# Attention by pairs of heads: a block mask carried in extra contraction rows, probabilities normalised before they are turned, values stationary on two column halves

## The reference

```python
for blk in range(S // Q_BLOCK):                       # Q_BLOCK = 128, CHUNK = 64
    q0 = blk * Q_BLOCK
    k_end = q0 + Q_BLOCK
    s = einsum('bqhd,bkhd->bhqk', q[:, q0:k_end], k[:, :k_end]) * scale
    mask = (arange(k_end) // CHUNK)[None, :] <= ((q0 + arange(Q_BLOCK)) // CHUNK)[:, None]
    s = where(mask, s, -inf)
    p = softmax(s, axis=-1)
    outs.append(einsum('bhqk,bkhd->bqhd', p, v[:, :k_end]))
```

## Time and profile before

| what | value |
|---|---|
| median of 3 runs | 4078.86 us (4068.8 to 4081.03) |
| span of the profiled execution, its only recorded time | 4081.4 us |
| TensorE busy in the span | 3546.4 us (87%) |
| VectorE busy | 1301.3 us (32%) |
| ScalarE busy | 776.8 us (19%) |
| mean granted TensorE clock | 0.926 |

### The profile page before, as it was taken

The page is one execution under the profiler, slowest core; times in us unless marked ns, Lnnn a source line. Parts: engine busy times, 40 slices in busy tenths (PEclk is TensorE's granted clock), DMA queues, the critical chain, the costliest instruction groups (busy, mean ns, idle before and its releaser), DMA issues. The chain is left out here.

```text
span 4081.4 us, 40264 instructions
## 1 busy us (share of the span) xinstructions
PE 3546.4 (87%) x12609; PEld 1976.0 (48%) x12610; DVE 1301.3 (32%) x1923; ACT 776.8 (19%) x1214; POOL 329.9 (8%) x600
## 2 busy tenths in 40 slices
PE   5999599979999996999778986947999999999862
PEld 2444255547676444444357762534444444444421
DVE  2222233344343123111246662253111111111155
ACT  2222123333333001111122220211111111111102
POOL 3100000000000000111110000001111111111042
PEclk9999799979898997999989998968999999999986
DMA  6910201221111210999631001106778977767474
GB/s 238 371 36 26 109 26 42 57 72 42 32 42 30 74 74 34 378 367 368 225 91 27 21 0 66 37 16 236 280 271 307 333 275 277 274 245 277 156 254 158
DMA packets 204249, 636.98 MB, mean 156 GB/s; under 512 B 35349, under 2 KB 97401, under 8 KB 167033
## 3 DMA queue, kind: packets, MB, share of 16 engines
q1 hardware_dynamic: 142808, 412.34, 28.8%
q0 software_dynamic: 43488, 158.35, 10.5%
q10 hardware_dynamic: 17856, 65.02, 3.9%
HBM read 492.00 MB, written 143.65 MB: 156 GB/s over the span
## 5 line engine op out<-in xcount | busy, mean ns | idle before, releaser
L1560 PE MATMUL gu_ps<-w_gu,x_t 128*128 x2016 | 891.0, 595 | 6.5 <-DVE x_t L1617 3.4
L1560 PEld LDWEIGHTS gu_ps<-w_gu,x_t 128*128 128x128 f32 x2016 | 375.9, 191 | 432.3 <-issue 432.3
L1581 PE MATMUL y_ps<-w_dn,hid_t 128*128 x992 | 446.3, 592 | 0.0
L390 PE MATMUL ps<-second,wcol 128*128 128x512 f32 x768 | 333.2, 596 | 9.9 <-DMA wcol<-in_w_in_dram 7.5
L1615 DVE TENSOR_TENSOR hid<-act_g,gu_ps 128x256 f32<-128x256 f32 x126 | 53.0, 421 | 873.7 <-ACT act_g L1597 873.7
L1581 PEld LDWEIGHTS y_ps<-w_dn,hid_t 128*128 128x128 f32 x992 | 179.1, 191 | 177.9 <-issue 177.9
L390 PEld LDWEIGHTS ps<-second,wcol 128*128 128x128 f32 x768 | 146.8, 191 | 195.4 <-issue 187.6
L1520 POOL COPY idx<-moe_slot_tok 128x1 int32 (+1 forms) x128 | 23.2, 181 | 2646.4 <-POOLq L94 1450.2
L1602 ACT ACTIVATE y<-y_ps 128x1024 f32<-128x1024 f32 x124 | 126.9, 1023 | 497.4 <-PE y_ps L1581 497.4
L1597 ACT ACTIVATE act_g<-gu_ps 128x256 f32<-128x256 f32 x126 | 48.4, 384 | 793.4 <-PE gu_ps L1560 793.4
L1545 PEld LDWEIGHTS x_ps<-ident,xb 128*128 128x128 f32 x1024 | 133.5, 189 | 91.4 <-issue 60.8
(11 more groups left out here) (406 smaller groups left out, 4127.3 us busy)
## 6 DMA issues: line engine op xcount, KB each, us to landing
w_gu<-in_w_gate_dram SPq DMA_DIRECT2D x96, 1024.0 KB, 8.0
w_gu<-in_w_up_dram SPq DMA_DIRECT2D x96, 1024.0 KB, 11.0
w_dn<-in_w_down_dram SPq DMA_DIRECT2D x96, 1024.0 KB, 13.4
expert_out<-y ACTq DMA_DIRECT2D x124, 512.0 KB, 9.7
expert_out<-zero POOLq DMA_DIRECT2D x94, 512.0 KB, 37.7
wcol<-in_w_in_dram SPq DMA_DIRECT2D x12, 1024.0 KB, 9.7
qk_by_head<-stage SPq DMA_DIRECT2D x32, 384.0 KB, 3.3
qk<-qk_by_head SPq DMA_DIRECT2D x16, 768.0 KB, 5.2
```

What stands on the lines that cost most here:

```text
L390: last = nc.tensor.matmul(ps[:, slot, c, h * BANK:(h + 1) * BANK], wcol[:, k, kc, c * P:(c + 1) * P], G.u[:, kc, h * BANK:(h + 1) * BANK], ...
L1560: last = nc.tensor.matmul(gu_ps[:, slot], x_t[:, slot, c, :], w_gu[:, bass.ds(ws, 1), :, c, :].rearrange("p o g n -> p (o g) n"), start=c ...
L1581: last = nc.tensor.matmul(y_ps[:, h * BANK:(h + 1) * BANK], hid_t[:, slot, c, :], w_dn[:, bass.ds(ws, 1), c, h * BANK:(h + 1) * BANK] .rea ...
```

## The change

Only `attention` changes, and its two neighbours are left alone.

1. The mask's matmul is gone. Eight rows are added below the 96 of queries and keys (`KROWS` = 104). Row r holds, on the query side, 1 for the first 64 queries of tile r and, on the key side, 1e30 for the last 64 keys of block r, and 0 elsewhere. GpSimd writes these rows at the start of the stage into all four buffers of `qk`: two fills and 16 selects. TensorE waits for all 18 before its first scores.
2. Heads are taken in pairs, tile by tile: wide of head A, narrow of A, wide of B, narrow of B. Scores of a wide tile are issued four steps ahead, of a narrow one two steps ahead. `qk` has four buffers (was two), values are loaded by pairs, `prob` and `prob_t` have more buffers.
3. VectorE normalises the probabilities before they are turned: a reciprocal of the step's sum and a multiply in place over the tile (`scale`), and TensorE's turn waits for it. The scaling, turning and copying of `o_rows` is gone.
4. In `values` the 64 value columns of a head are stationary and 128 turned queries move. Head A writes output partitions 0 to 63, head B 64 to 127, and their matmuls alternate. The result is already turned; ScalarE copies it to `G.yb` in two pieces per pair.

```diff
-            n = (ORDER[s % T] + 1) * P
+            n = (tile_of(s) + 1) * P
...
         def _(pool):
-            nc.gpsimd.memset(early[:, 0:CHUNK], 1.0).then_inc(cleared, 1)
-            nc.gpsimd.memset(early[:, CHUNK:], 0.0).then_inc(cleared, 1)
-            nc.gpsimd.memset(hide[:], -NEG).then_inc(cleared, 1)
+            g = nc.gpsimd
+            st = Steps(pool, cleared)
+            st(g.memset(qk[QK:KROWS, :, 0, :], 1.0))
+            st(g.memset(qk[QK:KROWS, :, 1, :], -NEG))
+            st.join()
+            for u in range(4):
+                for side, first in ((0, 0), (1, CHUNK)):
+                    x = qk[QK:KROWS, u, side, :]
+                    st(g.affine_select(out=x, in_=x, compare_op=ALU.is_ge, fill=0.0, base=-first,
+                                       pattern=[[1, S]], channel_multiplier=-P))
+            st.join()
...
-            pe.wait_ge(cleared, 3)
+            pe.wait_ge(cleared, 18)
...
-                        nc.tensor.matmul(out[:, c0:c0 + w], qk[:, u % 2, 0, t * P:(t + 1) * P],
-                                         qk[:, u % 2, 1, c0:c0 + w], start=True, stop=c0 + w < n)
-
-                    nc.tensor.matmul(out[:, n - CHUNK:n], early[:], hide[:], start=False, stop=True
-                                     ).then_inc(sc_ready, 1)
+                        last = nc.tensor.matmul(out[:, c0:c0 + w], qk[:, h % 4, 0, t * P:(t + 1) * P],
+                                                qk[:, h % 4, 1, c0:c0 + w], start=True, stop=True)
+                    last.then_inc(sc_ready, 1)
...
-                    pe.wait_ge(exp_done, j * N + (s + 1))
+                    pe.wait_ge(scaled, j * N + (s + 1))
...
                     for b in range(t + 1):
-                        last = nc.tensor.matmul(o_ps[:, t, :], prob_t[:, s % 2, b, :],
-                                                vv[:, u % 2, b, :], start=b == 0, stop=b == t)
+                        for a, of in ((0, s - 2), (1, s)):
+                            rows = slice(a * VH, (a + 1) * VH)
+                            last = nc.tensor.matmul(o_ps[rows, r, :], vv[:, p % 2, b, rows], turned_of(of)[:, b, :],
+                                                    start=b == 0, stop=b == t)
                     last.then_inc(o_ready, 1)
...
-                scores(0)
-                scores(1)
+                for s in range(3):
+                    scores(s)
                 for i in range(N):
                     turn_probs(i)
-                    if i + 2 < N:
-                        scores(i + 2)
-                    if i:
+                    if ahead(i) < N:
+                        scores(ahead(i))
+                    if i and (i - 1) % 4 >= 2:
                         values(i - 1)
-                    for kind, p in turns[b_no["probs", i] + 1:][:1]:
-                        if kind == "out" and i + 1 < N:
-                            turn_out(p)
                 values(N - 1)
-                turn_out(ROUND // 2 - 1)
...
+                def scale(s):
+
+                    one = slice(s % 8, s % 8 + 1)
+                    v.wait_ge(exp_done, j * N + (turn_no[s] + 1))
+                    d.reciprocal(inv[:, one], total[:, one]).then_inc(inv_ready, 1)
+                    v.wait_ge(inv_ready, j * N + (s + 1))
+                    d.tensor_scalar(prob_of(s), prob_of(s), inv[:, one], None, ALU.mult).then_inc(scaled, 1)
+
+                for s in range(3):
+                    tops(s)
+                scale(0)
+                for i in range(N):
+                    v.wait_ge(b_ready, j * N + (i + 1))
+                    if i >= 8:
+                        v.wait_ge(o_ready, j * VALS + (value_no(i - 8) + 1))
+                    t = tile_of(i)
+                    if i % 2 == 0:
+                        d.tensor_copy(turned_of(i)[:, 4:t + 1, :], turn_b[:, 0:t - 3, :]).then_inc(b_taken, 1)
+                        scale(i + 1)
+                        if i + 2 < N:
+                            scale(i + 2)
                     else:
-                        d.tensor_copy(prob_t[:, n % 2, 0:t + 1, :], turn_b[:, 0:t + 1, :]).then_inc(b_taken, 1)
-                    if n + 2 < N:
-                        tops(n + 2)
+                        d.tensor_copy(turned_of(i)[:, 0:t + 1, :], turn_b[:, 0:t + 1, :]).then_inc(b_taken, 1)
+                    if ahead(i) < N:
+                        tops(ahead(i))
```

More of the change, by code:

```diff
@@ L812, in attention, with head_of, tile_of, ahead @@
     ORDER = [7, 0, 6, 1, 5, 2, 4, 3]
+    PAIRS = ROUND // 2
     N = ROUND * T
[L815 to L824, removed]
-    with ph.ctx:
[L826 to L835, removed]
+    KROWS = QK + T
+    OUTS = 2 * PAIRS
+    VALS = PAIRS * T
+    def head_of(s):
+        return s // (2 * T) * 2 + s // 2 % 2
+    def tile_of(s):
+        return ORDER[s % (2 * T) // 4 * 2 + s % 2]
+    def ahead(s):
+        return s + 4 if s % 2 == 0 else s + 2
+    scored = [0, 1, 2] + [ahead(s) for s in range(N) if ahead(s) < N]
+    turn_no = {s: n for n, s in enumerate(scored)}
+    assert sorted(scored) == list(range(N))
+    with ph.ctx:
+        qk = ph.sb("qk", [KROWS, 4, 2, S])
+        vv = ph.sb("vv", [P, 2, T, 2 * VH])
+        prob_l = ph.sb("prob_l", [P, 2, S])
+        prob_s = ph.sb("prob_s", [P, 2, BANK])
+        prob_tl = ph.sb("prob_tl", [P, 4, T, P])
+        prob_ts = ph.sb("prob_ts", [P, 4, T // 2, P])
+        shift = ph.sb("shift", [P, 8])
+        total = ph.sb("total", [P, 8])
+        inv = ph.sb("inv", [P, 8])
         wide = ph.ps("wide", [P, 2, S])
@@ L878, in _ @@
+            for p in range(2):
+                for a in range(2):
+                    load(2 * p + a, 2 * p + a)
+                load_values(p, p)
             with sp.Fori(0, ROUNDS - 1) as j:
[L879 to L882, removed]
+                for p in range(PAIRS):
+                    reload(j, p)
+            for p in range(PAIRS - 2):
+                reload(ROUNDS - 1, p)
@@ L890, in _ @@
+            st.join()
+            for u in range(4):
+                for side, first in ((0, 0), (1, CHUNK)):
+                    x = qk[QK:KROWS, u, side, :]
+                    st(g.affine_select(out=x, in_=x, compare_op=ALU.is_ge, fill=0.0, base=first + CHUNK - 1,
+                                       pattern=[[-1, S]], channel_multiplier=P))
+            assert st.n == 18
         @block.tensor
         def _(pe):
-            pe.wait_ge(cleared, 3)
+            pe.wait_ge(cleared, 18)
@@ L917, in turn_probs @@
                         blocks = blocks[4:]
-                    pe.wait_ge(b_taken, 1 + j * B_ALL + b_no[what])
+                    pe.wait_ge(b_taken, 1 + j * N + s)
                     for b, src in enumerate(blocks):
@@ L935, in values @@
                     last.then_inc(o_ready, 1)
-                def turn_out(p):
-                    what = ("out", p)
-                    pe.wait_ge(o_taken, 1 + j * ROUND + (p + 1) * 2)
-                    pe.wait_ge(a_taken, 1 + j * A_ALL + a_no[what])
-                    for b in range(4):
-                        last = nc.tensor.transpose(turn_a[:, b, :], o_rows[:, b, :], G.ident[:])
-                    last.then_inc(a_ready, 1)
-                    pe.wait_ge(b_taken, 1 + j * B_ALL + b_no[what])
-                    for b in range(4):
-                        last = nc.tensor.transpose(turn_b[:, b, :], o_rows[:, 4 + b, :], G.ident[:])
-                    last.then_inc(b_ready, 1)
```

152 lines of the change are left out of this document (68 added, 84 removed).

## The result

| | before | after |
|---|---|---|
| median | 4079.95 us (4068.8 to 4091.2, 4 runs) | 3964.26 us (3961.66 to 3966.53, 4 runs) |
| stage, first scores to last copy to `yb` | 880.0 to 1321.5: 441.5 us | 898.0 to 1206.0: 308.0 us |
| a pair of heads at full clock | 49.9 us | 35.3 us |

The account below looks back on a forecast made before the run. TensorE, in its own program order, was taken to bound the attention stage. 8 x 37.2 + 12 (rounds) + 27 (clock) + 24 (start) = 361 us against 441.5, so -81: 3998 us, range 3970 to 4066.

Parts of the forecast that it names:

- eight pairs: Attention stage, eight pairs of heads at full clock: 37.2 us each after the change, where one took 49.88.
- two rounds, 12: Start and end of each of two rounds, with empty queues and last tiles uncovered: 6 us a round, where it was 3.
- half clock, 27: Time at 1.2 GHz in the changed stage: 61 us of it, losing 27 us.
- the start: TensorE waits for GpSimd's 18 mask-row writes before first scores: +24 us, bounds +18 and +39.
- The clock: I keep the share of half-clock time: Whole stage: half-clock share stays at 0.18, 79 of 441.5 us before, so 61 us at half lose 27.
- the case in which it stays away: Half clock absent from the stage but for its first 10 us: forecast 22 us lower, 3976.
- the walk: Waits followed along the engines' queues through all 16 steps of a pair: TensorE waits 3.0 us a pair.
- Side by side: Values product: the two column halves run beside each other, 7.7 us a pair in place of 15.4; chance 0.50.
- halves in turn: Values product: halves follow each other, 0.107 us a pass, 43.3 us a pair, 4048 us; chance 0.30 including partial overlap.
- The masks: Mask matmuls after the scores, 16 a pair at 0.56 us: removing them saves 9.0 us a pair.
- the lower bound, +18: Low end for the later first scores, which wait for GpSimd's fills and selects; +24 us was taken.
- slower by the clock: Rival for the stage: TensorE's longer gaps bring half clock oftener, up to 4217 us if all at half; chance 0.10.

## Why the prediction was wrong, step by step

The forecast gave 361 us for start and stage together, from 880; it took 326.0. The 35 us of the miss (34 between the forecast and the median), by terms:

| term of the sum | forecast | measured | off by |
|---|---|---|---|
| eight pairs | 8 x 37.2 = 298 | 8 x 35.3 = 282 | 15 |
| two rounds, 12, and half clock, 27 | 39 | 25.6 | 13 |
| the start | 24 | 18.0 | 6 |

**The step that failed** is "The clock: I keep the share of half-clock time". It put 61 us of the changed stage at half and 27 us of cost on them; there were 20.8 us, none inside a running pair, and as a microsecond at half can lose no more than half a microsecond of work, they cost at most 10.4. Before, the two stretches inside pairs had cost 25.8. Where the masks were the only thing taken out, the half clock fell from 80 to 19 us, and the stage by 27 us beyond the pairs. A share is not a property of a stage: it hung on what the change removed. The forecast had the case in which it stays away (22 us lower). The range's low end, 3970, has room for that and for the shorter start (6 us), and none for the shorter pairs (15 us), the second step that was mis-sized.

**The rounds** were not 12 us. Less the 10.4 that the half clock can have cost at most, the rest is still 15; so this term was too small, and it hid a part of the clock's error in the table's second line. With one round in place of two the rest falls by 16.0, to 9.6. Filling and emptying the queues once thus costs under 10, and the change of round 16, of which 7.2 are a standstill of TensorE (2.91 in the trace of before), 2.3 the wait for the first normalised tile, and at most 4.4 the half clock in which it works from 1053.5 to 1058.8 and from 1062.2 to 1065.6. The forecast's 6 us a round counted the first tile's wait and the emptying, and no longer standstill.

**A pair** has two terms off. The kernel without normalising gives TensorE's own work, 33.7 us where I had 34.2, and what VectorE adds, 35.3 - 33.7 = 1.6 where I had 3.0: over eight pairs 11 of the 15 us are the waits, which the walk made too long. The waits stand where they were forecast, at head B's narrow tiles and the handing over of `turn_b`, and the view of waits gives the loads 2.4 us there; a part of each is time that TensorE would lose anyway. VectorE is busy for 27.6 us, not 32.0. Its groups in the stage, against the earlier trace rows:

```profile
L1015 DVE TENSOR_REDUCE shift<-wide 128x1 f32<-128x1024 f32 (+3 forms) x64 | 65.1, 1018 | 51.3 <-PE wide L926 50.8
L1023 DVE TENSOR_SCALAR prob_l<-prob_l,inv 128x1024 f32<-128x1024 f32 (+3 forms) x64 | 41.8, 653 | 2.3
...
L1023 DVE TENSOR_SCALAR prob_s<-prob_s,inv 128x128 f32<-128x128 f32 (+3 forms) x64 | 24.7, 387 | 2.3
L1021 DVE RECIPROCAL inv<-total 128x1 f32<-128x1 f32 x128 | 20.0, 156 | 7.2 <-ACT prob_s L979 7.2
```

(41.8 + 24.7)/8 = 8.3 us a pair, as forecast. The reciprocals take 20.0/8 = 2.5 where I had 3.8, because I took their distance to an instruction that waits for them. With minima and copies as before that sums to 30.7; the 27.6 is the union of records, which overlap where instructions follow each other.

**The values** were right in kind. Side by side was taken, with 7.7 us of passes and 2.9 of changes, 10.6; measured are 144 x 0.055 = 7.9, and the 33.7 us of own work less scores, turned blocks and these passes (33.7 - 15.4 - 7.7 - 7.9) leave 2.7 for the eight groups, 0.34 each, of which the loads show 0.15 behind the group. That makes 10.6. The Trainium skill, "TensorEngine Tiling (Array Packing)", section Key Properties, says that tiles load and multiply in parallel and that a change of mode drains the engine: this trace agrees with both, with 0.055 us a pass and about 0.15 a change. The rival, halves in turn, was priced too high: 43.3 a pair against 40.0 measured. That the halves overlap where one takes over from the other is my reading of it, not a separate measurement.

**The masks** were put at 9.0 us a pair. Their own time is 8.1, and what a pair gains is 6.6, as TensorE then waits for what they had covered. The forecast took the idle time of before out (1.0) and counted the waits anew, so the second of these differences is no miss of the pair's sum. That the change of rows costs 0.35 of a mask's 0.56 is borne out by size: 0.26 to 0.30 a mask with full rows.

**The start**: the fill was right (7.0 us for two), the select 1.0 and not 1.4; the lower bound, +18, was the truth. The rival "slower by the clock" did not come: the gaps of the new order, 1.6 to 2.4 us in 35, brought no half clock.

**Open.** Why the kernel before ran at half clock for 2 x 27 us within its pairs. Both stretches begin at the same point of their round, 137.7 us after its first scores (1017.7 after 880.0, and 1239.5 after 1101.8), and TensorE is busy all through them (27.00 of 27.00 and 28.00 of 28.00 us in the earlier trace rows), so they seem to belong to the program's work and not to a wait. They need the one-row masks (with 128 rows, or none, they go), but the same masks in the changed order don't bring them. Which part of the changed order keeps them off was not separated: the order by pairs, the form of the values product and the normalising changed together. The forecast's total also covers a few microseconds by which starts of the stage differ between executions (875.0 and 878.0 in two kernels that leave everything ahead of the stage as it was).

## What to carry to other kernels

A stretch of half clock is a cost like any other and has to be assigned to something before a change is priced; a share of time carried over is a guess, and both its ends belong in the range together with those of the other terms. On TensorE a tiny matmul with one contraction row can cost several times its passes (0.56 us here, where its two passes of 64 columns would take 0.11 at the pace of the scores); put it into spare contraction rows, or pad it to the full height. Two products of half width paid here when consecutive instructions went to different halves (0.055 us a pass against 0.11), and a stage that runs as a hardware loop of few rounds should be tried as one (16.5 us here).

## What was not expected of the hardware

- Padding a one-row matmul with 127 rows of zeros made it cheaper: 45.7 us a pair against 49.9, and 1.5% on the median.
- The half clock went with one-row matmuls in one order of the program (80 us, and 24 with full rows). In another, adding them lengthened it from 21 to 38 us, but only at the start and around the change of round.
- The two long stretches of half clock began at the same point of both rounds, with TensorE busy throughout.
- Halves that were issued one after the other took about 0.4 us a group less than their passes in turn.
- The change of round of the loop stopped TensorE for 7.18 us with nothing shown as its cause, and left it at half clock behind it; in the order of before it stopped it for 2.91 us.
